# A decoder step on one core: query projection tile by tile, and the new rows' convolution on GpSimd

## The chip, the cores and the metric

The kernel runs on one core of one Trainium2 chip. The metric is the time of one execution on the device, in microseconds (us). A core has TensorE (matmuls), VectorE (DVE), ScalarE (ACT), GpSimd (POOL) and SyncE (SP), which run their own instruction streams and wait for each other with semaphores. SyncE and ScalarE also issue DMA transfers.

## The reference, cut to what matters

One layer of a hybrid decoder over 1024 prompt rows and 64 new rows (8 sequences of 8 tokens, "sample"), model width 1024. One input projection feeds two groups of heads:

```python
z = h @ w_in                       # u_val, u_gate, q, k, v, qi, ki, wi
u = u_val * sigmoid(u_gate)
q = rope_partial(rms_norm(q))      # 8 heads of 64
k = rope_partial(rms_norm(k))      # 4 heads of 64
...
full = concatenate([past_u, u])    # 30 rows of state, then the new ones
y = depthwise_conv(full, dw_w, width=31) + dw_b      # 512 channels
y = silu(layer_norm(y))
...
sel = top_k(indexer scores, 256)   # each query attends to its selected keys only
attn = softmax(q . k[sel] / 8) . v[sel]
x = x + concatenate([y, attn]) @ w_out
x = x + (silu(n @ w_gate) * (n @ w_up)) @ w_down     # n = rms_norm(x)
```

For the prompt, the past of the convolution is zero; for the new rows it is the state, and their keys and values lie in paged caches of 1024 rows for each of the 8 sequences.

## The kernel before, in words

**Stages.** Everything is float32, and large products are made of three matmuls of a high and a low part (`three`). In order: row norms and the gated convolution input `u` (to about 200 us of the trace); index queries and index scores (to 330); selection of the 256 keys by halving, with the key and value projection beside it (to 414); the query projection and the norms of keys and queries (to 476); attention, 64 heads of tiles (`n` = 8 x tile + head, 476 to 770); output projection and FFN (the rest, bound by TensorE).

**The projections** (`project`, L891) go by chunks `c`; chunk 4 is the query. A tile is 128 rows (the tile of the new rows, SAMPLE, has 64), its result one PSUM bank of 512 columns (tile t in bank t, SAMPLE in bank 4). For chunk 4 the order is that of `ALL`: SAMPLE, then 0 to 7, in three groups: SAMPLE; tiles 0 to 3; tiles 4 to 7. Within a group the contraction `k` is the outer loop. In the middle of the third group TensorE does `key_transposes` (L925), 16 transposes of the keys into banks 0 to 3, which wait until five query tiles have been evacuated and the keys are normed.

**ScalarE** evacuates tiles (`take_query`, L1631), squares them, and stores each, once VectorE has rotated it, to DRAM (`store_query`, L1648; `q_scratch`). A tile's buffer `qst` is one of three, so a tile's copy waits for the store three tiles back. `FIRST_LATE` = 5: five tiles are taken so during the projection, of the four others two (`TAKEN_EARLY`) right after it and two (`TAKEN_THEN`) behind the first query's transposes, into buffers of their own; their squares, norms and stores are strewn over heads 0 to 6. Between tiles 1 and 2 of that order ScalarE issues the four stores of the keys and values (L1666 to L1669). After the projection it copies the transposed keys out of PSUM (L1679), and VectorE makes their low parts (L2255).

**VectorE** (`norm_query`, L2201) sums the squares of each head and applies the rotation. The inverse root is GpSimd's (`query_inverses`, L773); a prompt tile's is applied later, in the mask line of the heads (L2273), only the new rows' query waits for it (L2211) and is scaled at once.

**SyncE** loads queries back from DRAM (`load_queries`, L626) in the order 0, SAMPLE, 1, 2, ...; TensorE transposes them (`query_transposes`, L1116) in the heads: SAMPLE's in head 2, tile i+1 in head 8i+5. The rows of the convolution were stored to DRAM earlier and come back (L667 to L671) once five query tiles are stored and the first new keys transposed.

**The heads.** For each n, TensorE computes scores (L1157, L1158), transposes of the weights two heads back (L1173) and values three heads back (L1185). VectorE adds the mask and takes the maximum (L2273), ScalarE does the exponential (L1700). In heads 8, 24, 40, 56 the paged attention of two sequences is mixed in (`sample_scores`, L1254), which needs the block `q_blk` that VectorE fills in head 4. Beside this VectorE works through a list of `fill` items, spread over heads 0 to 44 by the weight tile + 1: first 44 taps of the prompt's convolution (L1971, L1975), then eight items of the new rows' convolution (`sample_taps`, L1977: a product of 31 taps at once, L1987, and its sum, L1988). The layer norm over the convolution's output begins in head 46 (`layer_norm_sum`, L1204), and waits for all taps.

**GpSimd** splits the weights into high and low parts (L751, L753); between the query inverses and the layer norm it has nothing to do. It zeroes part of the query buffer (L812) after the projection.

Of the kernel before, what the change touches and what calls it, by code (L numbers as in the profile page):

```python
# [24 lines left out]
F32 = mybir.dt.float32  # L25
# [47 lines left out]
CHUNKS = [[], SEL, SEL, ALL, ALL]  # L73
# [11 lines left out]
HALVINGS = 11  # L85
JOIN = 5
# [12 lines left out]
FIRST_LATE = 5  # L99
TAKEN_EARLY = (8, 6)  # L100
TAKEN_THEN = (5, 7)
# [74 lines left out]
def decoder_program(nc, A, O):  # L176

    ctx = ExitStack()
    with ctx:
# [90 lines left out]
        hsq = at("hsq", 35904, [P, NH * HD])  # L270
# [13 lines left out]
        tap_p = at("tap_p", 25888, [P, NS // 2, TS, W])  # L284
# [36 lines left out]
        qst_late = at_w("qst_late", 28672, [P, 4, NH * HD])  # L321
        hsq_late = at_w("hsq_late", 38912, [P, 3, NH * HD])
# [199 lines left out]
        def query_tile(o):  # L522

            r = rows_of(ALL[o])
            if o < FIRST_LATE:
                return qst[0:r, o % 3, :], hsq[0:r, :]
            return qst_late[0:r, o - FIRST_LATE, :], hsq_late[0:r, (o - FIRST_LATE) % 3, :]

# [27 lines left out]
        def _(sp):  # L556
# [69 lines left out]
            def load_queries(place):  # L626
# [3 lines left out]
                o = ALL.index(i)  # L630
# [36 lines left out]
            sp.dma_start(u_a[0][:, :], u_scr[:, 0, :]).then_inc(u_back, 16)  # L667
            sp.dma_start(y[:, LATE, 0:S], y_scr[:, LATE, :]).then_inc(y_back[0], 16)
            sp.dma_start(u_a[1][:, :], u_scr[:, 1, :]).then_inc(u_back, 16)
            sp.dma_start(us_a[:, :, :], us_scr[:, :, :]).then_inc(u_back, 16)  # L670
            sp.dma_start(y[:, 0:LATE, 0:S], y_scr[:, 0:LATE, :]).then_inc(y_back[1], 16)  # L671
            load_queries(2)
            load_queries(3)
            load_queries(4)
            for pr in range(NS // 2):
                if pr > 0:
                    pages_now = page_numbers(sp, 2 * pr), page_numbers(sp, 2 * pr + 1)
                    if pr == NS // 2 - 1:
                        sp.wait_ge(tap_done, CT * W)
                        sp.wait_ge(stap_done, 3 * CT)  # L680
# [47 lines left out]
        def _(pool):  # L728
# [44 lines left out]
            def query_inverses(o):  # L773
                t = ALL[o]
# [5 lines left out]
                else:  # L780
                    power.then_inc(head_pow, 1)
                    pool.wait_ge(head_pow, o)
# [22 lines left out]
            for o in range(FIRST_LATE):  # L805
                query_inverses(o)
            pool.wait_ge(head_rs, FIRST_LATE + 1)
            pool.wait_ge(proj_done, BASE[5])
            for b in range(2):
                for kh in range(2):  # L810
# [3 lines left out]
            for o in range(FIRST_LATE, NT):  # L814
                query_inverses(o)
# [54 lines left out]
        def _(pe):  # L870
# [11 lines left out]
            def last_in_bank(c, t):  # L882

                if t == 4:
                    return BASE[c] + 1
# [5 lines left out]
            def project(c, n0, width_, evac):  # L891
# [3 lines left out]
                groups = [tiles[0:1], [t for t in tiles[1:] if t < 4], [t for t in tiles[1:] if t >= 4]]  # L895
                per = KT // 4
                for gi, group in enumerate(groups):
# [6 lines left out]
                    for k in range(KT):  # L904
                        if (c, gi, k) == (4, 2, KT // 2):
                            key_transposes()
                        n = n0 + k // per
# [9 lines left out]
                        if gi == 2 and k % per == per - 1 and k < KT - 1:  # L917
                            mm.then_inc(w_used, 1)
# [6 lines left out]
            def key_transposes():  # L925

                pe.wait_ge(proj_evac, BASE[4] + FIRST_LATE)
# [7 lines left out]
            def new_key_transposes():  # L935

                pe.wait_ge(proj_evac, BASE[4] + FIRST_LATE + 2)
# [3 lines left out]
                mm.then_inc(kt_ps, 1)  # L941

# [173 lines left out]
            def query_transposes(i):  # L1116
                place = QUERY_ORDER.index(i)
                pe.wait_ge(q_in[place % 2], 16 * (place // 2 + 1))
                if i == SAMPLE:
                    pe.wait_ge(qt_lo, 1)  # L1120
                elif i == 1:
                    pe.wait_ge(qt_ready, 2)
                elif i > 1:
# [1455 lines left out]
```

## Time and profile before

| | |
|---|---|
| three runs | 1682.42, 1684.09, 1685.3 us; median 1684.09 |
| profiled execution | 1683.43 us, span of its trace 1681.6 us |
| TensorE busy | 1545.2 us, 92% of the span |
| VectorE busy | 908.3 us, 54% |
| ScalarE busy | 426.5 us, 25% |
| GpSimd busy | 473.8 us, 28% |
| mean granted clock of TensorE | 0.954 |
| chain that ended last | TensorE 68%, VectorE 18%, issue 6%, ScalarE 4% |

A row of the trace gives a start or a count, a duration, an engine, a line of the kernel, and the tiles written and read; in square brackets stands the engine's idle time before it and what ended it. "Issue" is time in which an engine waited for nothing that the profile shows. PEclk is the granted clock of TensorE as a share of 2.4 GHz. The span of the trace is 1.8 us shorter than the execution's time.

### The profile page before, as it was taken

To read this page: it belongs to the slowest core of one execution; us is meant where nothing else is said; L and a number is where in the kernel's file an instruction comes from. 1 tells how busy PE (TensorE), PEld (TensorE's weight loads), DVE (VectorE), ACT (ScalarE), POOL (GpSimd) and SP (SyncE) were. 2 spreads that over 40 slices of the span, in tenths; PEclk is the share of its full clock that TensorE was granted. 3 is DMA by queue.
4 is the path that set the end of the run, shared out by engine and by line. 5 is a ranking of instruction groups with operands and counts; after the bars stand their busy time and mean duration, and the time that the engine had idled before them with its cause. 6 is when DMAs were issued, how large, how long until landed. Compare 5 with 4: busy or idle time off the path is not lost.

```text
span 1681.6 us, 24236 instructions
## 1 busy us (share of the span) xinstructions
PE 1545.2 (92%) x9069; PEld 1419.7 (84%) x9069; DVE 908.3 (54%) x1584; ACT 426.5 (25%) x781; POOL 473.8 (28%) x310
## 2 busy tenths in 40 slices
PE   4999988889857886899999999999999999999999
PEld 3998767547645665789999999999999999999999
DVE  6799879999646786453343423324143342423323
ACT  3200268754245543452231010000101001010000
POOL 4643111221320000013433343342433324343320
PEclk9999999999967887899999999999999999999999
DMA  6212100110243221023210111110111111111102
GB/s 201 82 45 71 56 13 26 50 51 26 84 148 113 84 86 51 26 63 145 76 50 26 43 45 50 37 50 25 62 37 50 37 37 50 40 48 50 37 0 106
DMA packets 68637, 100.16 MB, mean 60 GB/s; under 512 B 12017, under 2 KB 49137, under 8 KB 68431
## 3 DMA queue, kind: packets, MB, share of 16 engines
q1 hardware_dynamic: 63714, 94.32, 17.4%
q10 hardware_dynamic: 4853, 4.93, 0.9%
q8 instruction: 41, 0.67, 0.2%
q14 instruction: 29, 0.24, 0.0%
HBM read 86.57 MB, written 13.02 MB: 59 GB/s over the span
## 4 chain that ended last, share of the span: by engine, by line
PE 68%; DVE 18%; issue 6%; ACT 4%; DMA 1%; POOL 1%; SPq 0%; ACTq 0%; DVEq 0%; POOLq 0%
PE ps L878 20%; PE ps L880 20%; PE ps L879 20%; DVE y_e L1975 2%; DVE mcnt L2112 2%; PE ps L1185 2%; DVE y L1975 1%; PE ps L1173 1%; DVE sm L2273 1%; ACT rl L1561 1%; PE ps L1157 1%; PE ps L1313 1%; ACT lo_t L1693 1%; DMA xt<-in_x_t 1%; PE ps L1158 1%
## 5 line engine op out<-in xcount | busy, mean ns | idle before, releaser
L878 PE MATMUL ps<-hi_t,w_hi 128*128 128x384 f32 (+2 forms) x1464 | 479.6, 328 | 6.3 <-DVE lo_t L1891 3.9
L880 PE MATMUL ps<-hi_t,w_lo 128*128 128x384 f32 (+2 forms) x1464 | 478.7, 327 | 0.0
L879 PE MATMUL ps<-lo_t,w_hi 128*128 128x384 f32 (+2 forms) x1464 | 478.4, 327 | 0.0
L878 PEld LDWEIGHTS ps<-hi_t,w_hi 128*128 128x128 f32 (+1 forms) x1464 | 274.7, 188 | 8.6 <-POOL w_lo L753 2.9
L879 PEld LDWEIGHTS ps<-lo_t,w_hi 128*128 128x128 f32 (+1 forms) x1464 | 274.7, 188 | 0.5
L880 PEld LDWEIGHTS ps<-hi_t,w_lo 128*128 128x128 f32 (+1 forms) x1464 | 274.6, 188 | 0.6
L2501 DVE TENSOR_TENSOR x<-x,ps 128x384 f32<-128x384 f32 (+1 forms) x264 | 139.3, 531 | 106.4 <-PE ps L880 105.6
L878 PE MATMUL ps<-f_hi,w_hi 128*128 128x384 f32 (+1 forms) x528 | 175.5, 332 | 2.9 <-DVE x L2501 2.5
L879 PE MATMUL ps<-f_lo,w_hi 128*128 128x384 f32 (+1 forms) x528 | 172.9, 327 | 0.0
L880 PE MATMUL ps<-f_hi,w_lo 128*128 128x384 f32 (+1 forms) x528 | 172.8, 327 | 0.0
L861 POOL CAST w_hi<-w_raw 128x1024 fp32r<-128x1024 f32 x60 | 62.8, 1047 | 335.2 <-PE ps L880 335.2
L1837 ACT ACTIVATE sg<-sg 128x384 f32<-128x384 f32 (+1 forms) x66 | 33.3, 508 | 465.1 <-DVE sg L2477 465.1
L863 POOL TENSOR_TENSOR w_lo<-w_raw,w_hi 128x1024 fp32r<-128x1024 f32 x60 | 147.6, 2460 | 4.8
L2487 DVE TENSOR_TENSOR ff<-ps,sg 128x384 f32<-128x384 f32 (+1 forms) x66 | 35.4, 536 | 209.0 <-PE ps L880 208.1
L2477 DVE TENSOR_TENSOR sg<-ps,rs_all 128x384 f32<-128x384 f32 (+1 forms) x66 | 35.2, 535 | 202.0 <-PE ps L880 200.1
L751 POOL CAST w_hi<-w_raw 128x1024 fp32r<-128x1024 f32 (+1 forms) x39 | 47.9, 1229 | 255.3 <-PE ps L880 166.2
L1975 DVE SCALAR_TENSOR_TENSOR y_e<-u,kf,y_e 128x1024 f32<-128x1024 f32 x77 | 113.6, 1475 | 2.5
L878 PEld LDWEIGHTS ps<-f_hi,w_hi 128*128 128x128 f32 x528 | 98.9, 187 | 9.6 <-DVE x L2501 9.2
L878 PE MATMUL ps<-w_hi,hi_t 128*128 128x512 f32 (+1 forms) x256 | 100.8, 394 | 3.2 <-DVEq L2068 2.3
L843 POOL TENSOR_TENSOR sg<-sg,rs_all 128x384 f32<-128x384 f32 (+1 forms) x66 | 63.7, 966 | 141.3 <-ACT sg L1837 141.3
L753 POOL TENSOR_TENSOR w_lo<-w_raw,w_hi 128x1024 fp32r<-128x1024 f32 (+1 forms) x39 | 101.5, 2603 | 3.1
L879 PE MATMUL ps<-w_lo,hi_t 128*128 128x512 f32 (+1 forms) x256 | 100.0, 391 | 0.0
(314 smaller groups left out, 2342.7 us busy)
## 6 DMA issues: line engine op xcount, KB each, us to landing
w_raw<-in_w_gate SPq DMA_DIRECT2D x22, 512.0 KB, 3.4
w_raw<-in_w_up SPq DMA_DIRECT2D x22, 512.0 KB, 3.4
w_raw<-in_w_down SPq DMA_DIRECT2D x22, 512.0 KB, 3.5
w_raw<-in_w_in SPq DMA_DIRECT2D x16, 512.0 KB, 3.6
kt_b<-in_cache_kt SPq DMA_DIRECT2D x48, 128.0 KB, 2.3
v_b<-in_cache_v SPq DMA_DIRECT2D x48, 128.0 KB, 2.4
x<-in_x_t SPq DMA_DIRECT2D x8, 544.0 KB, 8.1
w_raw<-in_w_u SPq DMA_DIRECT2D x8, 512.0 KB, 3.6
```

The costliest lines, as they stand in the source:

```text
L751: pool.tensor_copy(w_hi[:, n % SLOTS, 0:w], w_raw[:, n % RAW, 0:w]).then_inc(split_hi, 1)
L753: pool.tensor_tensor(w_lo[:, n % SLOTS, 0:w], w_raw[:, n % RAW, 0:w], w_hi[:, n % SLOTS, 0:w].bitcast(F32), ALU.subtract).then_inc(split_l ...
L843: pool.tensor_tensor(sg[:, m % 3, 0:z - a], sg[:, m % 3, 0:z - a], rs_all[:, a:z], ALU.mult).then_inc(sg_ready, 1)
L861: pool.tensor_copy(w_hi[:, slot, :], w_raw[:, raw, :]).then_inc(split_hi, 1)
L863: pool.tensor_tensor(w_lo[:, slot, :], w_raw[:, raw, :], w_hi[:, slot, :].bitcast(F32), ALU.subtract).then_inc(split_lo, 1)
L878: pe.matmul(out, a_hi, b_hi, start=first, stop=False)
L879: pe.matmul(out, a_hi, b_lo, start=False, stop=False)
L880: return pe.matmul(out, a_lo, b_hi, start=False, stop=last)
L1975: dve.scalar_tensor_tensor(yp, up, w, yp, ALU.mult, ALU.add).then_inc(tap_done, 1)
L2477: dve.tensor_tensor(sg[:, m % 3, 0:z - a], ps[:, m % 3, 0:z - a], rs_all[:, a:z], ALU.mult).then_inc(gate_taken, 1)
L2487: dve.tensor_tensor(ff[:, m % 2, 0:z - a], ps[:, 3 + m % 3, 0:z - a], sg[:, m % 3, 0:z - a], ALU.mult).then_inc(f_ready, 1)
L2501: dve.tensor_tensor(x1[:, m, a:z], x1[:, m, a:z], ps[:, 6 + q % 2, 0:z - a], ALU.add).then_inc(y_added, 1)
```

## The change

**Query projection.** Chunk 4 now goes in the order 0 to 7, SAMPLE (`TILES`), each tile a group of its own. The key transposes stand ahead of tile 7 and wait for four evacuated tiles. Inside SAMPLE, after its first two `k`, stand the transposes of the new keys and those of query 0 (which wait for tile 7's evacuation). ScalarE takes tiles 0 to 6 during the projection, copies columns 0 to 895 of the keys, takes tile 7, and copies the last 128 columns; VectorE's low parts are split in the same way. SAMPLE's query is taken after query 0's copy, its sum stands in head 0, its norm in head 1, its store in head 2, its transposes in head 4, its copy in head 5, `q_blk` in head 6. The squares have two buffers instead of one. The key and value stores now stand behind the copy of tile 1 and ahead of the first query store. An exponential of one column stands ahead of the keys' squares. GpSimd's zeroing is done in two halves, the first after query 0's transposes.

**SyncE.** The convolution's rows come back when all eight prompt queries are stored, ahead of the second half of the first pages' keys and of SAMPLE's query.

**The new rows' convolution** leaves VectorE's list and stands on GpSimd after the last query inverse: for each of four channel tiles eight groups of four taps (the last of three), each a product over [8 sequences, 8 rows, taps], additions by halves, and an addition to the output (for the first group, to the bias).

```diff
-CHUNKS = [[], SEL, SEL, ALL, ALL]
+TILES = ALL[1:] + [SAMPLE]
+CHUNKS = [[], SEL, SEL, ALL, TILES]
+TAPS = 4
+TAP_GROUPS = [(w, min(w + TAPS, W)) for w in range(0, W, TAPS)]
+NEW_TAP_STEPS = CT * 4 * len(TAP_GROUPS)
-FIRST_LATE = 5
-TAKEN_EARLY = (8, 6)
-TAKEN_THEN = (5, 7)
+LATE_QUERY = NT - 1
...
@@ SyncE
             load_queries(0)
-            load_queries(1)
-            sp.wait_ge(kt_ps, 2)
-            sp.wait_ge(stores, 16 * 4)
-            load_keys(0, 1, pages_now[1])
             for r in range(3):
-                sp.wait_ge(q_out[r], 16 * len(range(r, FIRST_LATE, 3)))
+                sp.wait_ge(q_out[r], 16 * len(range(r, LATE_QUERY, 3)))
...
             sp.dma_start(u_a[0][:, :], u_scr[:, 0, :]).then_inc(u_back, 16)
+            sp.dma_start(us_a[:, :, :], us_scr[:, :, :]).then_inc(u_back, 16)
+            sp.dma_start(u_a[1][:, :], u_scr[:, 1, :]).then_inc(u_back, 16)
             sp.dma_start(y[:, LATE, 0:S], y_scr[:, LATE, :]).then_inc(y_back[0], 16)
-            sp.dma_start(u_a[1][:, :], u_scr[:, 1, :]).then_inc(u_back, 16)
-            sp.dma_start(us_a[:, :, :], us_scr[:, :, :]).then_inc(u_back, 16)
             sp.dma_start(y[:, 0:LATE, 0:S], y_scr[:, 0:LATE, :]).then_inc(y_back[1], 16)
+            sp.wait_ge(kt_ps, 2)
+            sp.wait_ge(stores, 16 * 4)
+            load_keys(0, 1, pages_now[1])
+            load_queries(1)
             load_queries(2)
...
@@ GpSimd
+            query_inverses(LATE_QUERY)
+            pool.wait_ge(head_rs, NT + 1)
+            pool.wait_ge(u_back, 48)
+            taken = 0
+            for ct in range(CT):
...
+                for w0, w1 in TAP_GROUPS:
+                    n = w1 - w0
...
+                    pool.tensor_tensor(tap_p[:, :, :, 0:n], window, taps, ALU.mult).then_inc(stap_done, 1)
+                    taken += 1
+                    while n > 1:
+                        h = n // 2
+                        pool.wait_ge(stap_done, taken)
+                        pool.tensor_tensor(tap_p[:, :, :, 0:h], tap_p[:, :, :, 0:h], tap_p[:, :, :, n - h:n], ALU.add
+                                           ).then_inc(stap_done, 1)
+                        taken += 1
+                        n -= h
+                    pool.wait_ge(stap_done, taken)
+                    more = ys if w0 > 0 else kf[:, K_CB + ct:K_CB + ct + 1].unsqueeze(1).broadcast_to([P, NS, TS])
+                    pool.tensor_tensor(ys, tap_p[:, :, :, 0], more, ALU.add).then_inc(stap_done, 1)
+                    taken += 1
...
@@ TensorE, project
+                if c == 4:
+                    groups = [[t] for t in tiles]
...
-                        if (c, gi, k) == (4, 2, KT // 2):
+                        if c == 4 and (group, k) == ([S // P - 1], 0):
                             key_transposes()
+                        if c == 4 and (group, k) == ([SAMPLE], 2):
+                            new_key_transposes()
+                            query_transposes(0)
...
@@ TensorE, key_transposes
-                pe.wait_ge(proj_evac, BASE[4] + FIRST_LATE)
+                pe.wait_ge(proj_evac, BASE[4] + 4)
...
@@ TensorE, heads
-                if n == 2:
+                if n == 4:
                     query_transposes(SAMPLE)
...
@@ ScalarE
             act.wait_ge(left_done, 1)
+            act.activation(stat[:, 1, 0:1], ones[:, 0:1], ACT.Exp)
             act.activation(hsq_k[:, 0:SAMPLE, :], k_tok[:, 0:SAMPLE, :], ACT.Square)
...
+            take_query(0)
+            take_query(1)
+            act.wait_ge(k_ready, 1)
...
+            store_query(0)
+            for o in range(2, S // P - 1):
+                take_query(o)
+                store_query(o - 1)
             act.wait_ge(kt_ps, 1)
+            act.wait_ge(proj_done, BASE[4] + S // P - 1)
+            take_keys(0, S - P)
+            take_query(S // P - 1)
+            store_query(S // P - 2)
+            take_keys(S - P, S)
...
+            store_query(S // P - 1)
+            take_query(LATE_QUERY)
...
+                if n == 2:
+                    store_query(LATE_QUERY)
+                if n == 5:
                     take_queries(SAMPLE)
...
@@ VectorE
+            for o in range(S // P - 1):
+                query_squares(o)
+                query_rotation(o)
...
+            key_lows(0, S - P, 0)
+            query_squares(S // P - 1)
+            query_rotation(S // P - 1)
+            key_lows(S - P, S, NKV)
...
             fill = [(conv_taps, q, q + 1) for q in range(QI_TAPS[9], CT * W)]
-            fill += [(sample_taps, ct, half) for ct in range(CT) for half in range(2)]
...
+                if n == 0:
+                    query_squares(LATE_QUERY)
+                if n == 1:
+                    new_query_norm()
-                if n == 4:
+                if n == 6:
                     sample_queries()
```

## Rows read from the trace of the kernel before

**Rows 1.** The chain that ended last, by line, from 484 to 660 us.

```profile
by line: issue 14.9%; DVE y L1975 11.0%; DVE sm L2273 7.1%; ACT lo_t L1693 6.4%; DVE y L1988 5.4%; DVE tap_p L1987 5.3%; PE ps L1313 4.5%; DMA us_a<-us_scratch 4.1%; PE ps L1157 3.7%; PE ps L1173 3.7%; PE ps L1185 3.7%; PE ps L1288 3.0%; PE
```

**Rows 2.** Busy time by stage: start:end, length, engines (instructions), PEclk, DMA share, GB/s.

```profile
430.00:440.00 10.00, 10.00 (x45) 8.26 (x44) 6.88 (x12) 0.48 (x2) 3.61 (x2) 1.00 0.00 0
...
480.00:490.00 10.00, 2.86 (x11) 2.10 (x11) 4.56 (x7) 7.08 (x14) 0.00 (x0) 0.50 0.94 334
```

**Rows 3.** Timeline of TensorE: start us, us, instruction, [idle before <-releaser].

```profile
414.01 0.44 PE L878 MATMUL ps<-w_hi,hi_t 128*64 128x512 f32 x1 [0.60 <-ACT k_tok L1596]
...
460.07 3.67 PE L931 MATMUL ps<-kf,k_tok 128*128 128x128 f32 x16 [7.67 <-ACT qst L1638]
...
485.03 0.44 PE L1157 MATMUL ps<-hi_t,lo_t 128*128 128x128 f32 x1 [7.88 <-DVE lo_t L2289]
...
504.16 1.93 PE L1269 MATMUL ps<-kt_b,q_blk 128*32 128x512 f32 x8
```

**Rows 4.** Timeline of ScalarE and its DMA queue (ACTq), 421 to 490 us.

```profile
421.89 1.92 ACT L1624 ACTIVATE hsq_k<-k_tok 128x2048 f32<-128x2048 f32 x1 [6.33 <-DVEq L2135]
...
449.38 0.60 ACTq L1666 DMA_DIRECT2D out_k_prompt<-k_tok  x1
...
476.52 4.51 ACT L1679 ACTIVATE hi_t<-ps,kf 64x1024 fp32r<-64x1024 f32 x4
481.06 2.40 ACT L1693 ACTIVATE lo_t<-ps 64x512 fp32r<-64x512 f32 x4
...
486.16 1.28 ACT L1700 ACT_TABLE_LOAD   x1 [1.30 <-DVE stat L2273]
```

**Rows 5.** One step of the chain of waits, 440 to 510 us: a store's landing.

```profile
454.29 4.98 DMA q_scratch<-qst
```

**Rows 6.** Timeline of VectorE, 440 to 510 us.

```profile
443.38 0.31 DVE L2198 TENSOR_TENSOR kf<-kf 128x144 f32<-128x144 f32 x1
...
446.63 0.68 DVE L2212 TENSOR_TENSOR qst<-qst,hk 64x512 f32<-64x512 f32 x1 [1.74 <-POOL hk L777]
...
464.72 0.17 DVE L2246 TENSOR_TENSOR smx<-kb,smneg 64x64 bf16<-64x64 bf16 x1
477.67 5.23 DVE L2255 SCALAR_TENSOR_TENSOR hi_t<-ps,kf,hi_t 64x1024 fp32r<-64x1024 f32 x4 [12.77 <-ACT hi_t L1679]
...
490.38 1.28 DVE L1975 SCALAR_TENSOR_TENSOR y<-u_a,kf,y 128x1024 f32<-128x1024 f32 x1 [4.30 <-DMA us_a<-us_scratch]
...
509.60 1.29 DVE L2364 TENSOR_REDUCE sst<-ps 128x1 f32<-128x1088 f32 x1 [0.82 <-PE ps L1270]
```

**Rows 7.** SyncE's queue (timeline), then DMA issues: KB each, us to landing.

```profile
481.83 0.34 SPq L667 DMA_DIRECT2D u_a<-u_scratch  x1
...
q_scratch<-qst ACTq DMA_DIRECT2D x1, 128.0 KB, 2.3
q_ld<-q_scratch SPq DMA_DIRECT2D x1, 128.0 KB, 2.9
```

**Rows 8.** What VectorE waited for, 511 to 655 us: total, times, longest.

```profile
DVE sm L2273 <- PE ps L1158: 17.4, 9, 4.1
```

**Rows 9.** Timeline of VectorE, heads 41 to 46.

```profile
624.94 1.01 DVE L2273 CUSTOM_DVE_ANT_0 sm<-ps,mneg,hk 128x768 f32<-128x768 f32 x1
...
627.17 1.18 DVE L1987 TENSOR_TENSOR tap_p<-us_a,kf 128x992 f32<-128x992 f32 x1
...
655.47 1.02 DVE L2273 CUSTOM_DVE_ANT_0 sm<-ps,mneg,hk 128x768 f32<-128x768 f32 x1 [1.28 <-PE ps L1158]
```

**Rows 10.** Timeline of GpSimd, three stages.

```profile
164.94 3.25 POOL L753 TENSOR_TENSOR w_lo<-w_raw,w_hi 128x1024 fp32r<-128x1024 f32 x1
...
403.79 2.39 POOL L753 TENSOR_TENSOR w_lo<-w_raw,w_hi 128x1024 fp32r<-128x1024 f32 x1
...
457.68 0.24 POOL L783 TENSOR_SCALAR hk<-hk 128x8 f32<-128x8 f32 x1
```

**Rows 11.** Source line L1975 from 166 to 167 us: duration min/median/max in ns.

```profile
L1975 DVE SCALAR_TENSOR_TENSOR y_e<-u,kf,y_e x1: 3298/3298/3298, 166.0 to 166.0; 128x1024 f32<-128x1024 f32 x1
```

More of the change, by code:

```diff
@@ L804, in _ @@
             key_inverses()
-            for o in range(FIRST_LATE):
+            for o in range(LATE_QUERY):
                 query_inverses(o)
-            pool.wait_ge(head_rs, FIRST_LATE + 1)
-            pool.wait_ge(proj_done, BASE[5])
+            pool.wait_ge(head_rs, LATE_QUERY + 1)
             for b in range(2):
+                if b == 0:
+                    pool.wait_ge(qt_ps, 1)
+                else:
+                    pool.wait_ge(proj_done, BASE[5])
                 for kh in range(2):
@@ L916, in project @@
                                 mm.then_inc(proj_done, 1)
-                        if gi == 2 and k % per == per - 1 and k < KT - 1:
+                        if gi == len(groups) - 1 and k % per == per - 1 and k < KT - 1:
                             mm.then_inc(w_used, 1)
@@ L941, in new_key_transposes, with query_transposes @@
                 mm.then_inc(kt_ps, 1)
+            def query_transposes(i):
+                place = QUERY_ORDER.index(i)
+                pe.wait_ge(q_in[place % 2], 16 * (place // 2 + 1))
+                if i == SAMPLE:
+                    pe.wait_ge(qt_lo, 1)
+                elif i == 1:
+                    pe.wait_ge(qt_ready, 2)
+                elif i > 1:
+                    pe.wait_ge(mixa_hi, i - 1)
+                    pe.wait_ge(mixa_lo, i - 1)
+                else:
+                    pe.wait_ge(proj_evac, BASE[4] + S // P)
+                r = rows_of(i)
+                for j in range(4):
+                    mm = pe.transpose(ps[:, 7, j * P:j * P + r], q_ld[0:r, place % 2, j * P:(j + 1) * P], ident[0:r, 0:r])
+                mm.then_inc(qt_ps, 1)
             def new_index_keys():
@@ L1670, in _ @@
[L1670 to L1680 removed]
+                act.dma_start(q_scr[TILES[o], 0:rows_of(TILES[o]), :], query_tile(o)[0]).then_inc(q_out[o % 3], 16)
@@ new lines, in take_keys @@
+            def take_keys(first, last):
+                for p in range(2):
+                    for kh in range(2):
+                        half = slice(kh * HD, (kh + 1) * HD)
+                        if first > 0:
+                            act.wait_ge(kt_lo, 2 * p + kh + 1)
+                        act.activation(k_st[half, 2 * p + kh, first:last], wide(2 * p, S, half)[:, first:last], ACT.Copy,
+                                       scale=kf[half, K_GQC:K_GQC + 1]).then_inc(kt_ready, 1)
@@ L2249, in _, with key_lows @@
             dve.sem_inc(masks_ready, 1)
-            for g in range(NKV):
-                half, other = (slice(x * HD, (x + 1) * HD) for x in (g % 2, 1 - g % 2))
-                dve.wait_ge(kt_ready, g + 1)
-                dve.scalar_tensor_tensor(k_st[other, g, :], wide(2 * (g // 2), S, half), kf[half, K_GQC:K_GQC + 1],
-                                         k_st[half, g, :].bitcast(F32), ALU.mult, ALU.subtract).then_inc(kt_lo, 1)
+            def key_lows(first, last, taken):
+                for g in range(NKV):
+                    half, other = (slice(x * HD, (x + 1) * HD) for x in (g % 2, 1 - g % 2))
+                    dve.wait_ge(kt_ready, taken + g + 1)
+                    dve.scalar_tensor_tensor(k_st[other, g, first:last], wide(2 * (g // 2), S, half)[:, first:last],
+                                             kf[half, K_GQC:K_GQC + 1], k_st[half, g, first:last].bitcast(F32),
+                                             ALU.mult, ALU.subtract).then_inc(kt_lo, 1)
+            key_lows(0, S - P, 0)
+            query_squares(S // P - 1)
+            query_rotation(S // P - 1)
+            key_lows(S - P, S, NKV)
             NA = NH * (S // P)
```

168 lines of the change are left out of this document (56 added, 112 removed).

## The prediction, made before the change was run

> **What bounds the kernel now.** I read the profile page first: TensorE holds 68% of the chain that ended last, nearly all of it projections that the change leaves alone. Then the windows by stage, for where TensorE is not full. While the projections run, ten microseconds hold 45 matmuls of 512 columns, 0.222 us each, at full clock; from 480 to 490 us it works 2.9 us of ten at half the clock [rows 2]. So the change can only act between 414 and 660 us. There I read the engines' timelines and the chain by line. Two stretches stand out.
>
> First the end of the query projection. It starts at 414.0 after a 0.6 us wait, stops half way through its last four tiles for 7.7 us until ScalarE has taken five tiles, and the first head's scores begin at 485.0, after another 7.9 us of waiting [rows 3]. VectorE then waits for the convolution's rows to come back and starts its first tap at 490.4 [rows 6].
>
> Second the heads. From 484 to 660 us the chain runs through VectorE's taps (11.0%), its new-row convolution (5.4% and 5.3%) and its mask line (7.1%) [rows 1]. From 511 to 655 us VectorE waits for scores 17.4 us [rows 8], little in 144: it is the bound, but not all of its work is path.
>
> **The change, part by part.** All positions are those of the profiled execution.
>
> *Tile by tile.* The same 24 matmuls per tile, so 5.4 us each. The first tile needs no fresh evacuation: about 0.6 us earlier. Seven tiles end near 451.5. The key transposes now need four tiles out. ScalarE's fourth tile reuses the buffer of the first, so needs its store landed. That store is queued behind the four key and value stores, which started at 449.4 because the new rows' query went first [rows 4]. Now they start when the keys are ready: 443.4 [rows 6], plus the table load of 1.28 us [rows 4] and its 0.2 us exponential, which now stand ahead of the key squares at 421.9 on this very chain. So they start at 444.9, take 4.2 us to issue, and the query store behind them lands some 5.0 us later, as the one after them does now [rows 5]: about 455. One copy (0.7 us) more, and TensorE resumes at 455.8: a pause of 4.3 us instead of 7.7. The table load does save its place at the first head, but that is covered by the wait for the first tap, so it gains nothing there.
>
> *The end opened up.* ScalarE takes tiles three to six as their stores land, until about 461.4, copies 7/8 of the keys (4.51 us for all [rows 4], so 4.0) and takes the last prompt tile at 466.1. TensorE, ahead of it, has paused some 1.6 us inside the new rows' tile, and ends the projection near 471, not 475.5. VectorE ends its seventh rotation near 463.1, then 2.5 us of flag and masks up to its last small operation [rows 6], then 7/8 of the key remainders (5.23 us for all [rows 6], so 4.5) to 470.2, the eighth tile 1.8, the small key remainders 1.1, the query's remainder 1.4 behind ScalarE's 2.40 [rows 4]: the first scores start at 474.9 instead of 485.0, **10.1 us earlier**. The zeroing of the query buffers is split in halves; GpSimd does either in about 1 us beside this.
>
> *The convolution's rows come back.* SyncE now waits for all eight prompt stores; the last goes out at 473.3 behind ScalarE's query copy and lands about 475.6 (2.3 us [rows 7]). Before, the loads began at 481.8 [rows 7] and the first tap 8.5 us later. With the same four transfers in the way, the tap begins at 484.0, **6.4 us earlier**. The other 3.7 us of the early start are lost in this wait. Queued behind it on VectorE: the second head's mask, the new rows' query, and so all of TensorE's next scores.
>
> *The new rows' query now goes last.* This is the step that gives the gain back. After the first tap comes its sum (0.9 us), the power on GpSimd (1.74 us of waiting [rows 6]), the norm and rotation (2.2 us from that row): about 490.5. Its store goes out with the third head's exponential, 491.3, lands 2.3 us later, and SyncE's load takes 2.9 [rows 7]: 496.6. TensorE stands at its transposes in head 4 until then, with the next scores queued behind. The transposes of tile 1 then wait for head 5's exponential and a copy, to 499.5. The block of new queries is filled in head 6, behind a mask and a tap: ready at 504.6. The first paged scores started at 504.2 [rows 3], so **0.5 us later than now**, against which three late tiles' rotations (5 us of VectorE) have already been taken away. Bounds: 4 us earlier if landings and pauses are short, 3 us later if GpSimd's reads hold up each small norm operation. I take +0.5 and carry it to VectorE's maximum at 509.6 [rows 6].
>
> *Taps respread over heads 8 to 40.* The eight new-row items leave the list of 52, so 44 taps are spread over the same weights: 34 instead of 41 fall here. 7 x 1.28 us [rows 6] = 9.0. The waits for scores are 12% of the time [rows 8] and shorter ones stand beside them, so I take eight tenths of it as path: **-7.2**.
>
> *The convolution of the new rows on GpSimd.* 32 groups (four channel tiles, eight groups of taps) of four operations: 256, 128, 64 and 64 elements a partition. No row shows this form. Between 0.24 us (8 elements) and 2.39 us (1024 elements, two inputs) [rows 10], I take 0.60, 0.35, 0.25, 0.25 by size, plus 0.08 for each link: 1.8 us a group, 58 us in all, from 488 to about 565 once taps stand in between. Due at head 46, near 643, so nothing waits for it. It costs through VectorE: a tap that meets a subtraction of GpSimd took 3.30 us [rows 11] instead of 1.28, and the subtraction 3.25 instead of 2.39 [rows 10]. The tap started 1.0 us into the subtraction [rows 10, 11] and so ended 1.1 us after it: it stood still for what was left of the other. So a tap loses the rest of one short operation, 0.3 us: 15 taps, **+4.5**. Bounds: nothing, and 1 us for each of 34 taps with long operations.
>
> The Trainium skill says it this way ("SBUF — State Buffer", Who interferes with whom): a VectorE instruction with two SBUF inputs and a GpSimd instruction that reads SBUF exclude each other for the whole instruction, whoever is first. The trace agrees. A sharing of bandwidth over GpSimd's 58 us would instead have slowed all taps in that time in proportion.
>
> *Heads 41 to 46.* From 624.9 to 655.5 VectorE does eight items of 1.18 us twice, plus small adds [rows 9]: 20 us. Instead it has the last 7 taps, 9.0 us. -11.3, less the waits that then show (1.3 us at head 46 [rows 9]): **-10**.
>
> Behind head 46 nothing changes but the position. **Sum: +0.5 - 7.2 + 4.5 - 10 = -12.2 us.** The profiled execution took 1683.4 us for a span of 1681.6, the median is 1684.1, so 1671.2 beside it and 1672 against the median.
>
> **The rivals.** *A, the early gain stays* (17%): the new rows' query comes in time, or TensorE holds its clock from 475 on. For it: the rotations of three late tiles are gone from heads 1 to 4. Against: six dependent steps with two trips through DRAM. It keeps 6.4 instead of losing 0.5: 1665.
>
> *B, VectorE is not the bound in heads 41 to 46* (12%): ScalarE and TensorE alternate, half of the 10 us comes. For it: the 17.4 us of waits. Against: 30.5 us for five heads is nearly unbroken VectorE work there [rows 9]. 1677.
>
> *C, contention takes all* (8%): GpSimd's operations with four-element rows take 1 us or more each, so that they last through all taps, and each of the 34 loses 0.5 us, or 17 in all in place of 4.5: 1684, no change.
>
> *D, slower* (5%): the same operations take so long that the layer norm at head 46 waits for them. From 488 to 643 there are 155 us, 4.8 us a group; below that nothing is lost here, above it each further microsecond a group costs 32. At 6 us a group (1.5 us an operation) it is +37 over the forecast: 1709. For it: no row bounds these forms from above but the 2.39. Against: size.
>
> **How the numbers follow.** The forecast has 58%. The range 1664 to 1680 takes A and B in and the bounds of the query's trip and of the taps' hold-up; C's upper part and D are left out, with the ends of the forecast's own spread. A measurement of this kernel can tell 0.2%, 3.4 us, from no change. Faster: 56 of the forecast's 58, A, B, a little of C: 0.87. Same: 0.07. Slower: 0.06.
>
> **What would show it.** Right: first scores (the line of L1157) about 10 us earlier, the first tap 6 us, the first paged scores within 3 us of 504; VectorE's masks 4 us apart in heads 41 to 45 instead of 7; some GpSimd-held taps of 1.5 to 2 us up to 565. Wrong: a long wait of the layer norm's sum for GpSimd (D), taps of 1.8 us throughout (C), or paged scores at 498 (A).

## The result and the profile after

The changed kernel took 1667.4 us (median of 8 runs, 1665.5 to 1675.0) against 1683.8 for the kernel before in the same batch (8 runs, 1678.7 to 1685.3): a ratio of 0.991, 95% interval 0.990 to 0.993, so **faster by 0.9%**. Two later batches repeated it, at 0.995 [0.993, 0.997] and 0.991 [0.988, 0.993]. The forecast was 1672 with a range of 1664 to 1680. The profiled execution took 1669.3 us for a span of 1667.5; the forecast for it was 1671.2.

The page's first part and the head of its chain, after:

```profile
span 1667.5 us, 24356 instructions
...
PE 1537.3 (92%) x9069; PEld 1412.7 (85%) x9069; DVE 896.5 (54%) x1568; ACT 428.1 (26%) x786; POOL 545.4 (33%) x438
...
PE 69%; DVE 17%; issue 6%; ACT 4%; DMA 2%; POOL 1%; SPq 0%; DVEq 0%; ACTq 0%; POOLq 0%
```

TensorE's share of the chain is what it was, so the gain is in what stands between its work. TensorE's timeline answers to [rows 3]; L1194 is the line of the first scores, L1306 that of the paged ones:

```profile
455.00 3.40 PE L966 MATMUL ps<-kf,k_tok 128*128 128x128 f32 x16 [3.39 <-ACT qst L1677]
...
474.65 0.30 PE L1194 MATMUL ps<-hi_t,lo_t 128*128 128x128 f32 x1 [3.35 <-POOL lo_t L815]
...
493.82 0.68 PE L992 MATMUL ps<-kf,q_ld 64*128 64x64 f32 x4 [3.13 <-DMA q_ld<-q_scratch]
...
502.55 1.94 PE L1306 MATMUL ps<-kt_b,q_blk 128*32 128x512 f32 x8 [3.15 <-issue]
```

The pause inside the projection is 3.4 us instead of 7.7 (forecast 4.3), and the first scores start at 474.65 (forecast 474.9, before 485.0). The new rows' query is back at 493.8, and the paged scores start at 502.6 instead of 504.2: of ten microseconds 1.6 are left there.

ScalarE's timeline and VectorE's, answering to [rows 4] and [rows 6]:

```profile
421.97 1.28 ACT L1659 ACT_TABLE_LOAD   x1 [6.30 <-DVEq L2151]
...
423.37 1.90 ACT L1660 ACTIVATE hsq_k<-k_tok 128x2048 f32<-128x2048 f32 x1
```

```profile
481.94 1.28 DVE L2007 SCALAR_TENSOR_TENSOR y<-u_a,kf,y 128x1024 f32<-128x1024 f32 x1 [6.49 <-issue]
...
485.86 0.68 DVE L2239 TENSOR_TENSOR qst_late<-qst_late,hk 64x512 f32<-64x512 f32 x1 [1.58 <-POOL hk L777]
486.58 0.85 DVE L2240 TENSOR_TENSOR qst_late<-qst_late,kf 64x384 f32<-64x384 f32 x1
...
500.21 2.13 DVE L2388 COPY q_blk<-q_t 64x64 f32<-64x64 f32 x8
...
507.49 1.29 DVE L2395 TENSOR_REDUCE sst<-ps 128x1 f32<-128x1088 f32 x1 [3.33 <-PE ps L1307]
```

The table load now stands ahead of the keys' squares. VectorE's maximum over the paged scores starts at 507.5 instead of 509.6.

**How executions are compared below.** Profiled executions differ by up to 11.5 us ahead of the edit: the keys' squares started anywhere from 419.7 to 431.2 us in kernels that are alike up to there, mostly through the rounds that select keys. So I count from the end of the selection: the start of the keys' squares (before: 421.9, [rows 4]), or of the table load where that directly precedes them (after: 422.0). In runs 7 and 8 the load falls into idle time before the end of the selection, and the count is again from the squares. The marks are the starts of VectorE's mask instruction (L2305 after) of heads 0, 8, 41, 46 and 63, read from its timeline in each run. All in us:

| kernel | head 0 | head 8 | 8 to 41 | 41 to 46 | 46 to 63 | head 63 |
|---|---|---|---|---|---|---|
| before | 63.8 | 89.2 | 113.9 | 30.5 | 103.7 | 337.3 |
| changed | 53.1 | 87.0 | 112.3 | 21.0 | 103.5 | 323.7 |
| changed, again | 53.4 | 87.0 | 112.2 | 21.1 | 102.2 | 322.5 |
| changed, third | 53.6 | 87.2 | 112.1 | 21.1 | 102.2 | 322.6 |
| no new-row convolution | 53.5 | 85.9 | 112.3 | 21.5 | 104.0 | 323.7 |
| convolution left on VectorE | 53.7 | 84.7 | 113.1 | 28.4 | 104.1 | 330.4 |
| only the convolution moved | 63.9 | 87.5 | 111.1 | 21.0 | 102.2 | 321.9 |
| taps from head 3 | 53.3 | 82.4 | 111.7 | 21.6 | 101.5 | 317.3 |
| the same, query load first | 53.3 | 83.8 | 111.7 | 21.7 | 101.5 | 318.8 |
| taps done by head 40 | 53.8 | 85.7 | 114.3 | 14.1 | 102.7 | 316.9 |
| table load early | 51.7 | 84.9 | 111.3 | 21.5 | 104.0 | 321.7 |
| three edits together | 51.9 | 79.3 | 114.7 | 13.8 | 103.3 | 311.1 |
| eight taps at once | 53.8 | 90.1 | 112.4 | 21.0 | 102.0 | 325.5 |

The three executions of the changed kernel agree within 0.5 us at head 0 to head 46 and within 1.3 behind it; a difference of 1 us in a stage before head 46 can be read.

Of 13.6 us, 9.5 come in heads 41 to 46, 2.2 by head 8 and 1.6 between. VectorE's timeline there, answering to [rows 9]: the masks of heads 41 to 44 are 5.9, 4.8 and 4.5 us apart with two taps between them, those of heads 44 to 46 3.3 and 2.5 us apart (before: 6.3 to 7.4 up to head 45).

```profile
621.21 1.01 DVE L2305 CUSTOM_DVE_ANT_0 sm<-ps,mneg,hk 128x768 f32<-128x768 f32 x1
...
624.58 2.60 DVE L2007 SCALAR_TENSOR_TENSOR y<-u_a,kf,y 128x1024 f32<-128x1024 f32 x2
627.10 1.01 DVE L2305 CUSTOM_DVE_ANT_0 sm<-ps,mneg,hk 128x768 f32<-128x768 f32 x1
...
628.37 2.59 DVE L2007 SCALAR_TENSOR_TENSOR y<-u_a,kf,y 128x1024 f32<-128x1024 f32 x2
...
642.24 1.02 DVE L2305 CUSTOM_DVE_ANT_0 sm<-ps,mneg,hk 128x768 f32<-128x768 f32 x1 [1.14 <-PE ps L1195]
```

GpSimd's timeline, the convolution of the new rows:

```profile
485.90 1.11 POOL L831 TENSOR_TENSOR tap_p<-us_a,kf 128x256 f32<-128x256 f32 x1
...
489.30 1.75 POOL L836 TENSOR_TENSOR tap_p<-tap_p 128x128 f32<-128x128 f32 x2
...
491.55 0.61 POOL L831 TENSOR_TENSOR tap_p<-us_a,kf 128x256 f32<-128x256 f32 x1
492.24 0.78 POOL L836 TENSOR_TENSOR tap_p<-tap_p 128x128 f32<-128x128 f32 x2
...
493.52 0.61 POOL L831 TENSOR_TENSOR tap_p<-us_a,kf 128x256 f32<-128x256 f32 x1
```

A group undisturbed is 1.97 us (491.55 to 493.52; forecast 1.8). All 32 run from 485.9 to 566.7, 2.5 us each (forecast end 565). What lengthens them is VectorE, as a pair of rows shows: the tap that began at 489.14 holds the pair of additions at 489.30 for 0.97 us over its usual 0.78.

### The profile page after: what moved, and what is told of

It is laid out like the page before. It is cut to its first block, busy times and chain, and to the rows that moved or that the text cites. A ratio compares the mean times of both kernels' runs of the same rounds, so it can differ in the third digit from the quotient of the medians.

```text
span 1667.5 us, 24356 instructions
## 1 busy us (share of the span) xinstructions
PE 1537.3 (92%) x9069; PEld 1412.7 (85%) x9069; DVE 896.5 (54%) x1568; ACT 428.1 (26%) x786; POOL 545.4 (33%) x438
## 4 chain that ended last, share of the span: by engine, by line
PE 69%; DVE 17%; issue 6%; ACT 4%; DMA 2%; POOL 1%; SPq 0%; DVEq 0%; ACTq 0%; POOLq 0%
PE ps L906 20%; PE ps L908 19%; PE ps L907 19%; DVE y_e L2007 2%; PE ps L1222 2%; DVE mcnt L2128 2%; PE ps L1210 1%; DVE y L2007 1%; PE ps L1194 1%; ACT rl L1596 1%; ACT lo_t L1730 1%; PE ps L1195 1%; PE ps L1350 1%; DMA xt<-in_x_t 1%; DVE sm L2305 1%
```

## The experiments

Times are medians of 4 to 12 runs; the ratios are to the kernel before in the same batch.

**1. The new rows' convolution left out, its place in time kept.** The output of the new rows' convolution is zeros here.

```
-    for ct in range(CT):  (32 groups of four operations on GpSimd)
+    for ct in range(CT):
+        pool.memset(y[:, ct, S:ROWS], 0.0).then_inc(stap_done, 1)
```

> The changed kernel with the new rows' convolution left out: GpSimd writes zeros in its place, which reads nothing from SBUF (the layer norm of the 64 new rows then works on zeros). Theory 1: what GpSimd's reads cost VectorE is small, since the taps took 1.36 us on average in the changed kernel instead of 1.28, 1.4 us over 17 taps and about as much on the small operations of the query's norm: 1 to 2.5 us less than the changed kernel, taps all at 1.28. Theory 2, the forecast's: a tap loses the rest of one short operation, 0.3 us, 4.5 us in all on the path: 4 to 5 us less.

1670.7 us, ratio 0.991 [0.989, 0.993]: no faster than the changed kernel. By stage it is 1.1 us ahead at head 8 and level from 8 to 46 (112.3 and 21.5). So GpSimd's 32 groups cost VectorE's path about one microsecond in all, and nothing that can be read in heads 8 to 40. Taps from 484 to 568 us by line, first in this kernel, then in the changed one, then in the kernel before (count | busy, mean ns | idle before):

```profile
L1985 DVE SCALAR_TENSOR_TENSOR y<-u_a,kf,y 128x1024 f32<-128x1024 f32 x17 | 21.8, 1280 | 6.2 <-issue 6.2
```

```profile
L2007 DVE SCALAR_TENSOR_TENSOR y<-u_a,kf,y 128x1024 f32<-128x1024 f32 x17 | 23.1, 1361 | 0.0
```

```profile
L1975 DVE SCALAR_TENSOR_TENSOR y<-u_a,kf,y 128x1024 f32<-128x1024 f32 x22 | 28.2, 1281 | 4.4 <-DMA us_a<-us_scratch 4.3
```

The hold-up is 0.08 us a tap (1361 less 1280), 1.4 us over 17 taps, where I had put 0.3 on each of 15. The microsecond at head 8 is in small operations instead. VectorE's timeline of this kernel, against the rows of L2240 and L2388 above:

```profile
491.36 0.55 DVE L2218 TENSOR_TENSOR qst_late<-qst_late,kf 64x384 f32<-64x384 f32 x1
...
504.27 1.21 DVE L2366 COPY q_blk<-q_t 64x64 f32<-64x64 f32 x8
```

The product is 0.55 us without GpSimd's work and 0.85 beside it, the eight copies 1.21 and 2.13.

**2. The convolution left on VectorE, the rest of the change made.**

```
+    fill += [(sample_taps, ct, half) for ct in range(CT) for half in range(2)]
```

> The new query stage alone: the new rows' convolution is back on VectorE at the end of its list. Theory 1: of the 10 us by which the first scores come earlier nearly all is lost by head 8 (2.1 us left in the changed kernel) and it stays at that: 2 to 4 us less than the kernel before. Theory 2: the gains add otherwise, the early start is worth its 6 to 8 us once VectorE has the old load again: 6 to 8 us less than before.

1680.4 us, ratio 0.997 [0.996, 0.999]. The rebuilt projection alone brings 4.5 us by head 8 (84.7 against 89.2), and heads 41 to 46 take 28.4. From the end of the selection head 63 comes 6.9 us earlier than before; the medians show 3.4.

Head 8 also comes 1.2 us earlier here than in run 1, where GpSimd does nothing. The two differ in where the third tap stands. With 52 items in the list it falls in head 5; with 44 it falls in head 6, ahead of the eight copies that fill the block of new queries. VectorE's timeline of this kernel, then of run 1:

```profile
505.21 0.35 DVE L2296 CUSTOM_DVE_ANT_0 sm<-ps,mneg,hk 128x128 f32<-128x128 f32 x1 [1.20 <-PE ps L1170]
...
506.15 1.21 DVE L2380 COPY q_blk<-q_t 64x64 f32<-64x64 f32 x8
```

```profile
502.14 0.35 DVE L2283 CUSTOM_DVE_ANT_0 sm<-ps,mneg,hk 128x128 f32<-128x128 f32 x1 [2.40 <-PE ps L1173]
...
502.42 1.28 DVE L1985 SCALAR_TENSOR_TENSOR y<-u_a,kf,y 128x1024 f32<-128x1024 f32 x1
```

The copies start 0.9 us behind the mask of head 6 here, and 2.1 us behind it in run 1 (504.27).

**3. Only the convolution moved, the projection as before.** The diff is the reverse: the kernel before, with `sample_taps` taken out of the fill and the GpSimd loop behind the last query inverses.

> The other half alone: the query stage is that of the kernel before, only the new rows' convolution goes to GpSimd, behind its last query inverse. Theory 1: heads 41 to 46 shrink by 9 to 10 us and heads 8 to 40 by 1 to 2: 10 to 12 us less than before. Theory 2, contention takes it: taps of 1.6 us and more, under 5 us less.

1673.0 us, ratio 0.992 [0.991, 0.994], not to be told from the whole change by the intervals. TensorE's timeline has the first scores where the kernel before had them, behind the same wait (execution's start of the squares: 424.8, so 2.9 us late as a whole):

```profile
488.00 0.44 PE L1186 MATMUL ps<-hi_t,lo_t 128*128 128x128 f32 x1 [7.88 <-DVE lo_t L2302]
```

Yet from the end of the selection head 63 is reached at 321.9 us, against 322.5 to 323.7 for the whole change. **The gain is the convolution's move; tile by tile and the opened end bring next to nothing on top of it.** Their 10.8 us at head 0 are 0.5 us at head 8 (87.5 against 87.0). The parts don't add up: by head 8 the projection alone brings 4.5 us (run 2) and the convolution's move alone 1.7, both together 2.2. On top of the rebuilt projection the move costs 2.3 us by head 8: 1.2 for the tap that now stands in head 6 (run 2, 84.7, against run 1, 85.9), and 1.1 for GpSimd's hold-up (run 1 against 87.0).

**4. Taps only from head 3.** The first tap, with its wait for the convolution's rows, stands ahead of the new rows' query on VectorE; here it stands behind it. It is the only tap that heads 0 to 2 have: by the weights the next two fall in heads 3 and 6. The late query's store counts on a semaphore of its own.

```
-    weight = [n // NH + 1 if n < CONV_HEADS else 0 for n in range(NA)]
+    weight = [n // NH + 1 if 3 <= n < CONV_HEADS else 0 for n in range(NA)]
```

> The changed kernel with no tap in heads 0 to 2, so that the wait for the convolution's rows no longer stands ahead of the new rows' query on VectorE (its store counts on a semaphore of its own). Theory 1: this wait (6.5 us) is what the early start is lost in. Heads 1 and 2 then follow at 476 to 480, the query is stored near 480 instead of 489, and the first paged scores come 4 to 6 us earlier: 4 to 6 us less than the changed kernel. Theory 2: the trips through DRAM and SyncE's queue hold the query anyway, since its load stands behind eight key loads that are issued up to 483.9: at most 2 us less.

1665.5 us, ratio 0.989 [0.987, 0.991]; by stage 4.6 us ahead of the changed kernel at head 8 and 5 to 6 at head 63 (one tap fewer lies ahead of head 8). The medians, 1665.5 and 1667.4, don't tell the two apart. The second mask no longer waits for the convolution's rows. The query is rotated by 481.6, 57.0 us after the squares began, where the changed kernel had 65.2; but its load goes out late. SyncE's queue of this kernel, then TensorE, then the store's time to landing, here and in the changed kernel (KB each, median us to landing):

```profile
488.01 6.72 SPq L634 DMA_DIRECT2D q_ld<-q_scratch  x4
```

```profile
490.60 0.69 PE L992 MATMUL ps<-kf,q_ld 64*128 64x64 f32 x4 [6.96 <-DMA q_ld<-q_scratch]
...
498.64 1.94 PE L1306 MATMUL ps<-kt_b,q_blk 128*32 128x512 f32 x8 [2.46 <-issue]
```

```profile
q_scratch<-qst_late ACTq DMA_DIRECT2D x1, 128.0 KB, 6.1
```

```profile
q_scratch<-qst_late ACTq DMA_DIRECT2D x1, 128.0 KB, 2.2
```

Of the 8.2 us, 4.4 arrive in the load's issue (63.4 against 67.8 us after the squares). The other 3.8 are the store's landing: issued at 481.94 it landed 6.1 us later, where the changed kernel's took 2.2. The page loads of the keys stand ahead of the query's load in SyncE's queue, but their last was issued by 484.9, and SyncE then waited another 3.1 us for this store. From 477 to 488 us the DMA engines were over 90% busy with the convolution's rows and the pages; the changed kernel's store went out at 489.0, when they were idle.

**5. The same, and the query's load ahead of the second page loads.**

```
+    load_queries(1)
     load_keys(0, 1, pages_now[1])
-    load_queries(1)
```

> No taps in heads 0 to 2, and in SyncE's queue the load of the new rows' query stands ahead of the eight loads of the first pages' keys. Theory 1: in the kernel with taps from head 3 alone the query's load still waited behind those key loads; ahead of them it comes 2 to 4 us earlier, and the first paged scores with it: counted from the keys' squares head 8 at 78 to 79 us instead of 81.0. Theory 2: the key loads, now behind the query's store, are themselves too late for the first paged scores, and head 8 stays at 81 or later.

1668.5 us, ratio 0.990 [0.988, 0.993]. It loses: head 8 at 83.8 instead of 82.4. SyncE's queue shows what stood behind the load's wait:

```profile
489.96 0.50 SPq L634 DMA_DIRECT2D q_ld<-q_scratch  x1
490.64 4.33 SPq L641 DMA_DIRECT2D kt_b<-in_cache_kt  x8
495.07 5.09 SPq L634 DMA_DIRECT2D q_ld<-q_scratch  x3
```

The load starts 2.4 us earlier, counted from the squares (61.0 against 63.4), since the store, with no page loads beside it, lands in 3.6 us instead of 6.1. But the eight page loads and the next query's load wait behind it, and TensorE waits 4.4 us for the next tile's query.

**6. Taps done by head 40.**

```
-CONV_HEADS = 45
+CONV_HEADS = 41
```

> The changed kernel with all 44 taps spread over heads 0 to 40 instead of 0 to 44. Theory 1: heads 8 to 40 are held by the alternation of TensorE, ScalarE and VectorE, not by VectorE's work, so 7 more taps (9 us) fit there at a cost of 1 to 3 us, and heads 41 to 46 (21.0 us) lose their 9 us of taps for a gain of 5 to 7: 3 to 5 us less than the changed kernel. Theory 2, the forecast's: VectorE is the bound in eight tenths of that time, the taps cost 7 us there and win 7 to 9 behind: 0 to 2 us less.

1666.6 us, ratio 0.990 [0.988, 0.992]; in the same batch the changed kernel had 0.995 [0.993, 0.997]. The seven taps save 7 us where they leave (21.0 to 14.1) and cost 2 where they come in (112.3 to 114.3): **a tap is worth 1.0 us in heads 41 to 46 and 0.3 us in heads 8 to 40**. Head 8 comes 1.3 us earlier (85.7) with as many taps ahead of it: the third one is back in head 5, as in run 2. VectorE's masks in heads 41 to 43 of this kernel stand 2.6 and 2.7 us apart, and one waits for TensorE:

```profile
623.37 1.01 DVE L2305 CUSTOM_DVE_ANT_0 sm<-ps,mneg,hk 128x768 f32<-128x768 f32 x1
...
625.92 1.02 DVE L2305 CUSTOM_DVE_ANT_0 sm<-ps,mneg,hk 128x768 f32<-128x768 f32 x1 [0.41 <-PE ps L1195]
...
628.62 1.02 DVE L2305 CUSTOM_DVE_ANT_0 sm<-ps,mneg,hk 128x768 f32<-128x768 f32 x1
```

**7. The table load ahead of the wait for the selection.**

```
-    act.wait_ge(left_done, 1)
     act.activation(stat[:, 1, 0:1], ones[:, 0:1], ACT.Exp)
+    act.wait_ge(left_done, 1)
```

> The changed kernel with the one-column exponential ahead of ScalarE's wait for the selection instead of behind it. Theory 1: the table load stood on the chain of the keys; now it falls into ScalarE's 6 us of idle time. Keys' squares and everything up to the first tap 1.4 us earlier: counted from the end of the selection, the first scores and head 8 about 1.4 us earlier, and so the time. Theory 2: the chain has slack behind it (the stores' landings), and under 0.5 us arrives at head 8.

1671.4 us, ratio 0.992 [0.990, 0.994], beside 0.995 [0.993, 0.997] for the changed kernel: the time doesn't tell them apart. ScalarE's timeline shows the load in its idle time:

```profile
422.36 1.28 ACT L1658 ACT_TABLE_LOAD   x1
...
428.61 1.92 ACT L1660 ACTIVATE hsq_k<-k_tok 128x2048 f32<-128x2048 f32 x1 [4.76 <-DVEq L2151]
```

From the end of the selection head 0 and head 8 come 1.4 and 2.1 us earlier, so by this one execution the load did stand on the path; but its selection ended 6.6 us later than the changed kernel's, which no edit explains.

**8. Edits 4, 6 and 7 together.**

> The changed kernel with the three edits that each won where they act: taps of the convolution only from head 3 on, none due after head 40, and the table load ahead of the wait for the end of the selection. Theory 1, the three stages are independent: counted from the end of the selection (the start of the keys' squares, less the table load where it stands in front), head 8 is at about 81.5 (the changed kernel 87.0, the tap edit alone 82.4), heads 8 to 41 take 114 (112.3 and 2 for the taps moved in), heads 41 to 46 take 14.2 (21.0) and heads 46 to 63 103: about 10 us less than the changed kernel after the selection, some 1659 us against 1667 to 1673 for it beside these runs. Theory 2, moving ten more taps into heads 3 to 40 makes VectorE the bound there: heads 8 to 41 take 118 or more, and of the 10 us no more than 6 stay.

1662.2 us (1659.0 to 1664.2), ratio 0.986 [0.984, 0.988], against 0.991 [0.988, 0.993] for the changed kernel in the same batch: the fastest of all. The stages add up: head 8 at 79.3, heads 41 to 46 13.8, and heads 8 to 41 at 114.7, not 118. By the weights heads 8 to 40 hold 42 taps here and 34 in the changed kernel, eight more and not the ten I had written: 2.4 us for eight is 0.3 each again. Head 63 is reached 11.5 us earlier than in the control; the medians show 5.1, and only so much is confirmed by the time. In the profiled executions the selection ended at 426.3 here and at 419.7 in the control, and no edit explains that.

**9. Eight taps at a time on GpSimd instead of four.**

```
-TAPS = 4
+TAPS = 8
...
-NEW_TAP_STEPS = CT * 4 * len(TAP_GROUPS)
+NEW_TAP_STEPS = CT * 5 * len(TAP_GROUPS)
```

> The changed kernel with the sampled rows' convolution on GpSimd in groups of eight taps instead of four: 16 groups of five operations (512, 256, 128, 64 and 64 elements), the same sum in another order. GpSimd's own time stays near 55 to 60 us, from 486 to about 565. Theory 1, the rest of the other engine's instruction is what is waited for, whoever came second: a tap that comes into one of the 512-element products (about 1.2 us each, three tenths of the time) loses half of it, so the taps from 484 to 568 have a mean near 1.5 us instead of 1.36 with some of 2 us or more, and heads 8 to 41 take the same 112 to 113. Theory 2, a tap is hardly ever the one that waits: the mean stays within 0.05 of 1.36, none is over 1.8, and GpSimd's products carry the wait (up to 2.4 us). Either way the time is within 2 us of the changed kernel's.

1670.8 us, ratio 0.991 [0.990, 0.993]. Each product covers twice the elements, and there are half as many. VectorE's taps, then its small operations, then GpSimd; then a tap and the product that it met:

```profile
L2007 DVE SCALAR_TENSOR_TENSOR y<-u_a,kf,y 128x1024 f32<-128x1024 f32 x17 | 24.9, 1464 | 6.5 <-issue 6.5
```

```profile
488.19 1.46 DVE L2240 TENSOR_TENSOR qst_late<-qst_late,kf 64x384 f32<-64x384 f32 x1
...
503.24 2.83 DVE L2388 COPY q_blk<-q_t 64x64 f32<-64x64 f32 x8
```

```profile
491.64 2.48 POOL L831 TENSOR_TENSOR tap_p<-us_a,kf 128x512 f32<-128x512 f32 x1
...
496.30 1.22 POOL L831 TENSOR_TENSOR tap_p<-us_a,kf 128x512 f32<-128x512 f32 x1
```

```profile
544.60 2.23 DVE L2007 SCALAR_TENSOR_TENSOR y<-u_a,kf,y 128x1024 f32<-128x1024 f32 x1
```

```profile
544.46 1.28 POOL L831 TENSOR_TENSOR tap_p<-us_a,kf 128x512 f32<-128x512 f32 x1
```

The taps' mean rises to 1464 ns (0.18 us over the undisturbed 1280 instead of 0.08), near the 1.5 of the first theory, with one of 2.2 us: it began 0.14 us into a product and lost 0.95. Heads 8 to 41 do not notice (112.4). Head 8 does: 90.1 instead of 87.0, because the small operations on the query's way through VectorE are held longer. With the run without the convolution this is a series: 0.55, 0.85 and 1.46 us for the same product, 1.21, 2.13 and 2.83 for the copies, and 85.9, 87.0 and 90.1 at head 8.

**10. The changed kernel again, twice, as a control.**

> The changed kernel as it is, as the control of this set on the same chip. Counted from the start of the keys' squares, head 8's mask comes at 85.6 us, head 41's 112.3 us later and head 46's 21.0 us after that, within 1 us each; what varies between executions lies ahead of the keys' squares.

> The changed kernel once more, as the control of this batch. From the start of the keys' squares: first mask 51.8, head 8 85.6, heads 8 to 41 112.3, heads 41 to 46 21.0, heads 46 to 63 103 us, each within 1 us; its time within 5 us of 1668, and the start of the keys' squares anywhere from 420 to 431 us, since that lies ahead of the edit.

1673.0 us, ratio 0.995 [0.993, 0.997], and 1667.3 us, ratio 0.991 [0.988, 0.993]. The rows of the table agree; the medians of one and the same kernel are 5.7 us apart. A single ratio here is less certain than its interval says, and the 0.2% that the prediction took as enough to tell two kernels apart is not enough. The stages are what tells edits of a few microseconds apart, from one execution each outside the control.

## Why the prediction was right, and where it was not

The total held: 1667.4 against 1672, inside the range of 1664 to 1680. Part of that is luck, since two wrong terms nearly cancelled. The steps in its order:

*The end opened up: right.* The first scores came at 474.65 against 474.9, through the chain as written, pause and key copies included, with GpSimd's zeroing as the last of the waits by the profile (3.35 us). One remark failed: the table load was said to gain nothing because a later wait covers it. In run 7, without it on the way, heads 0 and 8 came 1.4 and 2.1 us earlier, in one execution.

*The convolution's rows: right in mechanism.* The first tap came at 481.9 where I had 484.0. The last prompt query's store was issued at 471.6, not 473.3.

*The new rows' query gives the gain back: right, a size off.* The maximum was at 507.5; I had 509.6 plus 0.5. The 2.6 us are the earlier first tap and a store and load landing in 2.2 and 2.6 us. The step "now goes last" is confirmed by runs 3 and 4: without the rebuilt projection head 8 is 0.5 us later, and taking the first tap from its way gives 4.6. GpSimd's hold-up of the small operations, for which I had a bound of 3 us, is 1.1 with four taps (run 1) and 4.2 with eight (90.1 against 85.9).

*Taps respread, -7.2: this is the term that was mis-sized.* "I take eight tenths of it as path" failed. Measured -1.6 with GpSimd at work, the same -1.6 without it (run 1), and -2.8 in run 3, for 9.0 us of taps: two to three tenths; run 6 gives 0.3 us a tap the other way round. I read the waits for scores, 12% of the time, as all that was not path. But the time that taps leave turns into longer waits. VectorE's waits from 511 to 568 us, before, then after:

```profile
DVE sm L2273 <- PE ps L1158: 9.2, 6, 2.9
```

```profile
DVE sm L2305 <- PE ps L1195: 13.9, 8, 3.1
```

Four taps fewer (16 instead of 20) are 3.9 us less of work there with GpSimd's hold-up in it, and the wait grew by 4.7. A nearer share stood in [rows 1]: L1975 holds 11.0% of 176 us on the chain, 19.4 us, and the 44 taps are 56 us of work, so a third of each is path, somewhat more than the two to three tenths measured. For the new rows' items on the same row it is 5.4% and 5.3%, 18.8 us of some 20: nine tenths, and there -10 came out as -9.5. (The sum's -11.3 should have been -11.0, 20 less 9.0; the -10 doesn't hang on it.)

*Contention, +4.5: the second mis-sized term.* Nothing measurable in heads 8 to 40, 1.1 us ahead of head 8. I had priced a tap that comes into a GpSimd operation, not how seldom that is, nor that the path share of a tap applies to its hold-up too: the taps' 1.4 us at a third of path are half a microsecond. Both errors have one root, and that they nearly cancelled was luck: -7.2 + 4.5 is -2.7, measured -1.6. The Trainium skill ("SBUF — State Buffer", Who interferes with whom) says that the one who starts first keeps the shared ports for the whole instruction, and the trace agrees that one waits for the other's whole rest, in both directions: in run 9 the tap that began 0.14 us into a 1.28 us product took 2.23, and another product, 1.22 us alone, took 2.48 where it met a 1.27 us tap. By the recorded starts that second product was first (491.64, the tap 491.77), so which of the two comes first is not shown by the starts. The same page ("SBUF: two separate sides") counts a VectorE instruction in a two-port mode among them, an f32 copy inside SBUF being one; the copies of the query block, one input each, were held (1.21 to 2.13 us), and the prediction had left them out by speaking of two inputs only.

*The rivals.* A (the early gain stays): it does not, but under run 4's order head 8 comes 6.8 us earlier than before. B (half of the 10 us): no, 9.5. C (contention takes all): no, 0.08 us a tap. D (GpSimd late at head 46): the convolution ends at 567, some 75 us ahead, at 2.5 us a group; 4.8 was the limit.

What stays open: why the convolution's move gained 1.7 us by head 8 under the old projection, why heads 41 to 46 took 28.4 us and not 30.5 with the convolution left on VectorE, why heads 46 to 63 vary from 101.5 to 104.1, and what makes the selection end up to 11.5 us apart. GpSimd's zeroing as the wait before the first scores was not taken away by itself.

## What to carry to other kernels

Price a piece of work that is moved off an engine by its share of the chain, not by the engine's busy or idle share: the chain by line, divided by the work of that line in the stretch, gave a third for the taps and nine tenths for the new rows' items; the runs measured two to three tenths and nine tenths. It is an average over the stretch: the same tap was worth 0.3 us in heads 8 to 40 and 1.0 in heads 41 to 46. In the stretch where VectorE also waited for scores, work taken out mostly lengthened the wait. And when work is pulled forward by ten microseconds, ask what the next item on each queue waits for: here a tap that waited for rows from memory stood ahead of the query that everything else needed, and moving that one tap behind it gave 4.6 us by head 8, where the rebuilt projection had added 0.5 to the convolution's move. The trip itself then got longer: the query's store, sent while the DMA engines were full, took 6.1 us to land instead of 2.2.

## What the runs showed of the hardware

GpSimd's two-input f32 operations on 128 partitions took 0.34 us for 64 elements a partition, 0.61 to 0.76 for 256 and 1.22 to 1.30 for 512. Many short ones beside VectorE were mostly held themselves (2.5 us a group instead of 1.97) and cost its long instructions little (0.08 us a tap); doubling the product's length raised that to 0.18, and it weighed most on VectorE's own short ones (0.55 to 0.85 to 1.46 us). A table load on ScalarE was 1.28 us, and the squares behind it started 1.4 us after it. The store of one 64-row query to DRAM landed in 2.2 us with idle DMA engines and in 6.1 us with full ones.
